# A two-layer diffusion block on one core: the opening re-ordered, GpSimd's arithmetic moved to VectorE, a ring of eight split weight blocks

## What is computed

```python
silu_c, silu_cc = silu(c), silu(c_ctx)
mod   = silu_c  @ w_ada[l] + b_ada[l]      # 2048 -> 3 * 2048: shift, scale, gate
mod_c = silu_cc @ w_ada[l] + b_ada[l]
h  = rmsnorm(x,  norm_g) * (1 + scale)   + shift
hc = rmsnorm(xc, norm_g) * (1 + scale_c) + shift_c
u, v_a, g_a, cq, ckv, kr, g_b, q_c, k_c, v_c, g_c = split_in(h @ w_in)
```

## Time and profile before

| | before |
|---|---|
| runs, us | 1631.42, 1628.64, 1631.72; median 1631.42 |
| profiled execution, span, us | 1630.7 |
| median of the runs less that span, us | 0.7 |
| PE busy | 1526.5 us, 94% |
| DVE busy | 1180.9 us, 72% |
| ACT busy | 684.2 us, 42% |
| POOL busy | 216.7 us, 13% |
| mean granted clock of TensorE | 0.979 |

### The profile page before, as it was taken

How to read it: one execution, slowest core, us unless ns; L and a number is a source line. 1 busy time by engine, 2 the same in 40 slices (tenths; PEclk the granted TensorE clock), 3 DMA queues, 4 the chain that set the end, 5 groups by cost and what they waited for, 6 DMA issues and landing times.

```text
span 1630.7 us, 26688 instructions
## 1 busy us (share of the span) xinstructions
PE 1526.5 (94%) x8082; PEld 1293.1 (79%) x8082; DVE 1180.9 (72%) x2080; ACT 684.2 (42%) x1274; POOL 216.7 (13%) x318
## 2 busy tenths in 40 slices
PE   3688899989999999999999999789989999999998
PEld 2456688878888888877888888678879988888897
DVE  3899788777978974757678887675765656767765
ACT  3766522242332323335462222343545534445554
POOL 1433321102111210100001110021200010200000
PEclk9799999999999999999999999899999999999999
DMA  8778676606665653642106775367736665731374
GB/s 238 241 249 261 232 251 183 191 27 199 174 189 154 209 152 91 173 117 57 42 12 208 240 234 172 95 151 188 240 121 178 172 181 137 229 91 46 106 213 145
DMA packets 318055, 268.62 MB, mean 165 GB/s; under 512 B 37072, under 2 KB 269712, under 8 KB 316944
## 3 DMA queue, kind: packets, MB, share of 16 engines
q1 hardware_dynamic: 296208, 196.23, 42.0%
q0 software_dynamic: 21760, 71.32, 13.7%
HBM read 257.00 MB, written 10.49 MB: 164 GB/s over the span
## 4 chain that ended last, share of the span: by engine, by line
PE 77%; DVE 11%; issue 4%; ACT 3%; DMA 2%; SPq 2%; DVEq 0%; POOL 0%; ACTq 0%; POOLq 0%
PE ps L916 23%; PE ps L918 23%; PE ps L917 23%; DVE w_lo L1305 4%; PE ps L921 2%; DMA ada_w<-in_w_ada 2%; PE ps L1077 1%; SPq L325 1%; ACT w_hi L567 1%; PE ps L1082 1%; PE ps L1081 1%; DVE ada_acc L1360 1%; DMA w_raw<-in_w_ada 1%; DVE prob L1508 1%; SPq L351 1%
## 5 line engine op out<-in xcount | busy, mean ns | idle before, releaser
L567 ACT ACTIVATE w_hi<-w_raw 128x512 fp32r<-128x512 f32 x656 | 406.9, 630 | 603.4 <-PE ps L918 533.6
L1305 DVE TENSOR_TENSOR w_lo<-w_raw,w_hi 128x512 fp32r<-128x512 f32 x656 | 472.0, 734 | 258.7 <-ACT w_hi L567 254.7
L916 PE MATMUL ps<-h_hi,w_lo 128*128 128x512 f32 (+1 forms) x1120 | 390.9, 349 | 3.4 <-DVE vc_lo L1319 1.5
L918 PE MATMUL ps<-h_hi,w_hi 128*128 128x512 f32 (+1 forms) x1120 | 388.2, 347 | 0.0
L917 PE MATMUL ps<-h_lo,w_hi 128*128 128x512 f32 (+1 forms) x1120 | 388.2, 347 | 0.0
L1360 DVE SCALAR_TENSOR_TENSOR ada_acc<-ada_w,c_silu,ada_acc 128x512 f32<-128x512 f32 x448 | 318.4, 747 | 8.9 <-DMA ada_w<-in_w_ada 8.6
L523 POOL DMA_DIRECT2D ada_w<-in_w_ada x256 | 137.4, 537 | 984.7 <-DVE ada_acc L1360 974.9
L916 PEld LDWEIGHTS ps<-h_hi,w_lo 128*128 128x128 f32 x1120 | 212.0, 189 | 31.9 <-issue 3.1
L918 PEld LDWEIGHTS ps<-h_hi,w_hi 128*128 128x128 f32 x1120 | 212.0, 189 | 26.3
L917 PEld LDWEIGHTS ps<-h_lo,w_hi 128*128 128x128 f32 x1120 | 212.1, 189 | 26.0
L1025 PE MATMUL ps<-w_lo,c_st 128*128 128x512 f32 x128 | 62.3, 487 | 36.5 <-DVE w_lo L1305 36.3
(11 more groups left out here) (220 smaller groups left out, 2375.9 us busy)
## 6 DMA issues: line engine op xcount, KB each, us to landing
w_raw<-in_w_in SPq DMA_DIRECT2D x336, 256.0 KB, 3.3
ada_w<-in_w_ada POOLq DMA_DIRECT2D x256, 256.0 KB, 3.6
w_raw<-in_w_ada SPq DMA_DIRECT2D x128, 256.0 KB, 4.2
w_raw<-in_w_out SPq DMA_DIRECT2D x128, 256.0 KB, 4.1
w_raw<-in_w_ukv SPq DMA_DIRECT2D x32, 256.0 KB, 3.1
ada_w<-in_w_in POOLq DMA_DIRECT2D x16, 256.0 KB, 3.9
x_scratch<-z SPq DMA_DIRECT2D x4, 1024.0 KB, 7.6
w_raw<-in_w_uq SPq DMA_DIRECT2D x16, 256.0 KB, 2.9
```

What stands on the lines that cost most here:

```text
L567: act.activation(dst, src, ACT.Copy).then_inc(hi_made, 1)
L916: pe.matmul(dst, a_lo, b_hi, start=first, stop=False)
L918: return pe.matmul(dst, a_hi, b_hi, start=False, stop=last)
L1305: dve.tensor_tensor(dst, src, top.bitcast(F32), ALU.subtract).then_inc(lo_made, 1)
```

## The change

- SP: w_ada blocks 0 to 7 are requested ahead of x and ctx, blocks 8 on right behind them; `load_bias(0)` comes behind v_c's rows.
- Ring: w_ada blocks use 8 split slots (`split_at`: w_hi/w_lo and the new wx_hi/wx_lo), `ADA_RING` = 8; ACT and DVE run `ADA_AHEAD` = 6 blocks ahead, 3 after the opening (`lead`, `led`).
- x: squares, turning and scaling start at block 10 (`X_AT`), the RMS matmul comes at block 20 (`RMS_AT`).
- Chunks: `normed` and xn are gone. DVE's `chunk_scaled` makes tmp = z * a_col * prob at step c (two instructions 128x256), ACT's `chunk_hi` h_hi from tmp and q_whi at c+1, DVE's `chunk_lo` h_lo (two 128x256) and q_wlo at c+3, PE's `q_unit` for the same chunk at c+4, c in (6, 13, 20, 27). The last four chunks and q_units are woven into the first blocks of v_c.
- POOL issues transfers only; the loads of q_c's rows start when x has landed. The mask is one DVE `min` with a table of the largest float or -1e30, behind v_c in both layers.
- The first ada block is added four steps later within v_c; its last four rows come behind the loop.
- The row copy goes to prob row 1 instead of tmp row 3. Groups are Python loops instead of `Fori` loops.

The diff, cut:

```diff
-CHUNK_AT = (4, 11, 18, 25)
+ADA_UNITS = 2 * KT * GROUPS
+ADA_RING, ADA_AHEAD = 8, 6
+CHUNK_AT = (6, 13, 20, 27)
+X_AT, RMS_AT = 10, 20
+def lead(u):
+    return max(min(u + ADA_AHEAD, ADA_UNITS - 1), u + AHEAD)
+def led(u):
+    return range(lead(u - 1) + 1, lead(u) + 1)
...
+        def split_at(u):
+            if u < ADA_UNITS and u % ADA_RING >= RING:
+                return wx_hi[:, u % RING, :], wx_lo[:, u % RING, :]
+            return w_hi[:, u % RING, :], w_lo[:, u % RING, :]
...
# SP
-            for tt in range(4):
-                src = (x if tt < 2 else ctx_in)[0, (tt % 2) * P:(tt % 2 + 1) * P, :]
-                sp.dma_start(x_in[:, tt, :], src).then_inc(x_landed[tt], 16)
...
-            for n in range(RAW):
-                ada_row(0, n)
-            load_bias(0)
...
+            for u in range(RAW):
+                ada_row(u)
+            for tt in range(4):
+                src = (x if tt < 2 else ctx_in)[0, (tt % 2) * P:(tt % 2 + 1) * P, :]
+                sp.dma_start(x_in[:, tt, :], src).then_inc(x_landed[tt], 16)
+            for u in range(RAW, ADA_UNITS):
+                ada_row(u)
...
                         sp.dma_start(x_scratch[:, 4 * g:4 * g + 4, :], z[:, 4 * g:4 * g + 4, :]).then_inc(x_kept, 16)
+                    load_bias(l)
...
# POOL: mask_bias, normed and q_lo are gone
+            pool.wait_ge(x_landed[3], 16)
+            for k in range(KT):
+                q_row(k)
...
# ACT
+                ring = ADA_RING if u < ADA_UNITS else RING
+                if u >= ring or per:
+                    act.wait_ge(unit_done, u - ring + 1 + per * i)
...
+            def chunk_hi(k):
+                act.wait_ge(t_ready, k + 1)
+                for v in range(2):
+                    t = slice(v * SEQ, (v + 1) * SEQ)
+                    ins = act.activation(h_hi[:, k, t], tmp[:, k % 2, t], ACT.Identity, bias=mods[:, v, k:k + 1])
+                ins.then_inc(op_hi, 1)
+                act.wait_ge(ada_in[k % 4], 16 * (k // 4 + 1))
+                if k >= 2:
+                    act.wait_ge(q_done, k - 1)
+                act.activation(q_whi[:, k % 2, :], ada_w[:, k % 4, :], ACT.Copy).then_inc(q_hi_made, 1)
+            for u in range(ADA_AHEAD):
+                prep(u)
+            for u in range(ADA_UNITS):
+                g, n = divmod(u, 2 * KT)
+                for ahead in led(u):
+                    prep(ahead)
+                if n % KT == 0 and u:
+                    rows_copy(g, n // KT)
+                if u in (X_AT, X_AT + 1):
+                    x_square(u - X_AT)
+                if 0 <= u - X_AT - 2 < KT:
...
+                if g and n - 1 in CHUNK_AT:
+                    chunk_hi(4 * g - 4 + CHUNK_AT.index(n - 1))
...
# PE
+                pe.matmul(ps[:, bank, :], c_st[:, s, :], top, start=False, stop=s == KT - 1).then_inc(unit_done, 1)
+                if g and n - 4 in CHUNK_AT:
+                    q_unit(4 * g - 4 + CHUNK_AT.index(n - 4))
             turn_rows_of(GROUPS, 0)
-            for c in range(5):
-                q_unit(GROUPS, c)
...
+                    if l == 0 and 1 <= k < 5:
+                        q_unit(KT - 5 + k)
...
# DVE
+            def chunk_scaled(k):
...
+                if k >= 2:
+                    dve.wait_ge(op_ready, k + 1)
+                for v in range(2):
+                    t = slice(v * SEQ, (v + 1) * SEQ)
+                    ins = dve.scalar_tensor_tensor(out=tmp[:, k % 2, t], in0=z[:, k, t], scalar=a_col[:, v, k:k + 1],
+                                                   in1=prob[:, 0, t], op0=ALU.mult, op1=ALU.mult)
+                ins.then_inc(t_ready, 1)
+            def chunk_lo(k):
+                dve.wait_ge(t_ready, k + 1)
+                dve.wait_ge(op_hi, k + 3)
...
+                dve.wait_ge(q_hi_made, k + 1)
+                dve.tensor_tensor(q_wlo[:, k % 2, :], ada_w[:, k % 4, :], q_whi[:, k % 2, :].bitcast(F32), ALU.subtract)\
+                    .then_inc(q_lo_made, 1)
...
+                if g and n in CHUNK_AT:
+                    chunk_scaled(4 * g - 4 + CHUNK_AT.index(n))
+                if g and n - 3 in CHUNK_AT:
+                    chunk_lo(4 * g - 4 + CHUNK_AT.index(n - 3))
...
+                    chunk_scaled(KT - 4)
                     for k in range(KT):
+                        if k < 4:
+                            if k < 3:
+                                chunk_scaled(KT - 3 + k)
+                            chunk_lo(KT - 4 + k)
                         prep_ahead(PLAN["v_c", l]["unit"] + k)
+                        if k == 4:
+                            block = ada_block(l, "v_c")
+                        if k >= 4:
+                            ada_add(block, k - 4)
+                        if 8 <= k < 12:
+                            lo(qc_lo[:, k - 8, :], ps[:, k - 8, :], qc_hi[:, k - 8, :], C_SCALE).then_inc(free[k - 8], 1)
+                    for k in range(KT - 4, KT):
                         ada_add(block, k)
...
                 ada(l, "v_c")
+                dve.wait_ge(bias_in, 16 * ROWS * HEADS_C * (l + 1))
+                near = bias[:, :, :].rearrange("p a (r c) -> p (a r) c", c=GRID_W)
+                dve.tensor_tensor(near, near, cst[:, C_MASK:C_MASK + GRID_W].unsqueeze(1).broadcast_to([P, 32, GRID_W]),
+                                  ALU.min).then_inc(bias_ready, 1)
```

More of the change, by code:

```diff
@@ L604, in _, with x_square @@
                 hi(c_st[:, :, 2 * v], c_silu[:, v * KT:(v + 1) * KT])
-            for c in range(2):
+            def x_square(c):
                 act.wait_ge(x_landed[c], 16)
@@ L659, in _ @@
+            rows_copy(GROUPS, 0)
             hi_n[0] += KT
@@ L661, in _ @@
             t_n[0] = KT
-            act.wait_ge(q_done, KT)
-            for j in range(4):
-                hi(qc_hi[:, j, :], ps[:, j, :], C_SCALE)
             def softmax_exp(j, keys):
@@ L1419, in _ @@
                                               1.0, 0.0, ALU.mult, ALU.add, small[:, 50 + c:51 + c]))
-            for u in range(AHEAD):
+            for u in range(ADA_AHEAD):
                 prep(u)
@@ L1439, in columns_of @@
                                              op0=ALU.add, op1=ALU.mult).then_inc(group_ready, 1)
[L1441 to L1447 removed]
+            def chunk_scaled(k):
+                if k % 4 == 0:
+                    dve.wait_ge(group_ready, k // 4 + 1)
+                if k == 0:
+                    dve.wait_ge(free[7], 1)
+                    for j in range(4):
+                        dve.wait_ge(free[j], KT // 4)
+                if k >= 2:
@@ L1480, in _ @@
-            group(0, 0)
-            group(1, 2 * KT)
-            with dve.Fori(2, GROUPS) as g:
-                group(g, 4 * KT, g - 2, 2 * KT)
+                for v in range(2):
+                    t = slice(v * SEQ, (v + 1) * SEQ)
+                    ins = dve.scalar_tensor_tensor(out=h_lo[:, k, t], in0=tmp[:, k % 2, t], scalar=mods[:, v, k:k + 1],
+                                                   in1=h_hi[:, k, t].bitcast(F32), op0=ALU.add, op1=ALU.subtract)
+                ins.then_inc(op_ready, 1)
@@ new lines, in chunk_lo, with x_scale @@
+                dve.wait_ge(q_hi_made, k + 1)
+                dve.tensor_tensor(q_wlo[:, k % 2, :], ada_w[:, k % 4, :], q_whi[:, k % 2, :].bitcast(F32), ALU.subtract)\
+                    .then_inc(q_lo_made, 1)
+            def x_scale():
+                dve.wait_ge(sq_ready, 2)
+                link(dve.tensor_scalar(small[:, 0:4], small[:, 50:54], 1.0 / D, EPS, ALU.mult, ALU.add))
+                rsqrt(4)
+                for c in range(4):
+                    ins = dve.tensor_scalar(tmp[:, 2, c * P:(c + 1) * P], ident, small[:, 10 + c:11 + c], None, ALU.mult)
+                    if c % 2:
+                        ins.then_inc(sq_sum, 1)
@@ new lines, in _ @@
+            for u in range(ADA_UNITS):
+                g, n = divmod(u, 2 * KT)
+                for ahead in led(u):
+                    prep(ahead)
+                if u in (X_AT, X_AT + 2):
+                    x_square(2 + (u - X_AT) // 2)
+                if u == X_AT + 5:
+                    x_scale()
+                if u == RMS_AT + 3:
+                    dve.wait_ge(job_done, 3)
+                    dve.tensor_copy(prob[:, 0, :], ps[:, 7, :]).then_inc(free[7], 1)
+                if n % KT == 5 and u > KT:
+                    columns_of(g, n // KT)
+                if g and n in CHUNK_AT:
+                    chunk_scaled(4 * g - 4 + CHUNK_AT.index(n))
+                if g and n - 3 in CHUNK_AT:
+                    chunk_lo(4 * g - 4 + CHUNK_AT.index(n - 3))
@@ L1484, in _ @@
             columns_of(GROUPS, 0)
-            for c in range(4):
-                chunk(GROUPS, c)
             hi_n[0] += KT
@@ L1489, in _ @@
             t_n[0] = KT
-            for j in range(4):
-                lo(qc_lo[:, j, :], ps[:, j, :], qc_hi[:, j, :], C_SCALE).then_inc(free[j], 1)
             def nmax(j, keys):
```

245 lines of the change are left out of this document (71 added, 174 removed).

## The result

The changed kernel takes **1667.62 us** (median of 4 runs, 1667.12 to 1668.65) against 1631.57 of the kernel before on the same chip (4 runs, 1628.64 to 1632.32): ratio 1.0221, 95% interval 1.0204 to 1.0239. It is slower, by 36 us. The profiled execution has a span of 1665.2 us against 1630.7; its mean granted clock is 0.963. DVE is busy for 1152.4 us and PE for 1536.9 us, 92% of the span, of which some is the same work at half rate.

A forecast was written before the change was run, and what follows sets the result against it. PE was taken as the bound after the opening, so what the opening gains or loses is kept. Terms -26.9 +26.9 +24.2 +0.5 +7.9 -4.3 = +28.3 on the 1630.7 span gave 1659 us, range 1632 to 1674.

The forecast's parts named there:

- rival A: Main case, all terms as summed: loops longer and clock lowered; 1659 us, own range 1647 to 1670, chance 0.60.
- half rate all through q_unit: Opening loops: the lower clock covers every q_unit whole, +41.5 us, 1672 us in all; chance 0.10.
- The mechanism of the loops: Opening loops: each chunk starts only when the last q_unit is over, and q_unit waits for its own chunk; plus 26.9 us.
- The chain: Path from q_unit round to the next: 10.8 us per ordinary loop, 14.3 per long one; eleven loops 125.8 against 98.9.
- Rival D: Opening loops: ACT and DVE get a chunk ahead of PE, loop 6.94 us, no pauses; 1592 us, chance 0.16.
- The clock term: Opening loops: PE's 4.8 us pauses bring the lower clock, 2.2 us eleven times; plus 24.2 us, ends 0 and 37.
- Rival B: Opening loops: equally long, but pauses too short to lower the clock; 1635 us, chance 0.14.
- The lead-in: Start up to q_unit 0: it comes at 59.1 against 86.0; minus 26.9 us, bounds -22 and -31.
- block 8 starts 26.0 us earlier: Lead-in: bias transfers moved back and x behind eight w_ada blocks, so block 8 is split by 21.3 us.
- The end of v_c: Value projection's end: PE's transposes wait 5.6 us for late ada sums, lower clock costs 2.3; plus 7.9 us; bias issues covered.
- Layer 1: Mask moved from POOL to DVE: stretched h_lo and PE's wait go; minus 4.3 us, ends 0 and -5.
- the rest of v_c: From q_unit 11 to the projection's end: 59.2 us against 58.7 now; plus 0.5 us.

The follow-up runs named there:

- the runs with 5, 4 and the late q_unit: Changed kernel with ADA_AHEAD 5 in place of 6: 1635.31 us; with 4: 1617.94 us; with 6 but q_unit behind block c+9: 1619.24 us.
- filling the pause: Changed kernel with 14 unused matmuls added on PE ahead of each q_unit but the first: 1647.53 us.
- The new opening in its best form: Changed kernel with ada sums spread, bias issued by POOL, x squares early, 5 blocks ahead and q_unit behind block c+6: 1605.49 us (4 runs).

## Why the prediction was right, and where it was off

It gave 1659 (1632 to 1674) and slower a chance of 0.77, chiefly by rival A (0.60): the ring that does not uncouple. The time is 1667.6, within the range; 1635 for "the clock stays up", 1672 for "half rate all through q_unit" and 1592 for "the ring uncouples" stood beside it.

**The mechanism of the loops was right.** It said that each chunk can only start when the last q_unit is over, since split c+13 has the slot of block c+5. The rows at 125.49, 125.98 and 126.64 show that hand-over, and the runs with 5, 4 and the late q_unit remove it. The chain was put at 10.8 us and 14.3; without the clock's part it is 10.48 and 14.13. One part was off: PE's pause was put at 4.8 us in each loop and is 2.1 to 4.9, since PE, at the lower clock, is busy for more of the loop than was counted. Rival D, that DVE would get ahead of PE, needed the slot to be no obstacle: with a lead of 4 it is none, and the loop is then 8 us, not D's 6.9, and does little better than the old one.

**The clock term was mis-sized a little:** +24.2 predicted, 19.9 measured by filling the pause. Rival B (no clock term) falls with it: the pauses did bring the lower level. With the clock kept up the time is 1647.53, where B had 1635, because other terms were put too low. By the Trainium skill, "TensorE: Matmul & The Clock Gate", part on the clock gate, the prediction had this term under 16 us. That does not hold here: 19.9 us are 1.2% of the span.

**The lead-in was the term that failed:** -26.9 predicted, with bounds of -22 and -31, and -19.1 measured, outside the bounds. Block 8 came at 24.38 instead of 21.3: 3.1 us. The windows view of the kernel after, over the stretch in which x and block 8 arrive (columns as above):

```profile
2.50:8.00 5.50, 0.58 (x2) 0.29 (x2) 1.24 (x5) 1.59 (x5) 0.34 (x1) 1.00 0.95 311
8.00:15.00 7.00, 6.23 (x16) 3.79 (x16) 4.78 (x8) 3.79 (x6) 0.00 (x0) 1.00 1.03 401
15.00:22.00 7.00, 0.00 (x0) 0.00 (x0) 0.00 (x0) 0.00 (x0) 0.00 (x0) 0.79 1.00 414
```

The prediction let 399 GB/s run from 2.5 us on. That rate is there from 8 us, and even exceeded, but the first 5.5 us have 311, which is 0.5 MB or 1.2 us less. By 22 us 7.4 MB had moved, more than the 6.9 of tables, eight blocks and x and the 0.25 of block 8, and ACT could copy block 8 only at 22.97. So transfers requested behind it had part of the rate; that is inferred from the sum, no run changes it. Block 32 came at 53.6 instead of 47.3, another 3.2 us late; there PE waits 5.15 us for z behind ACT's squares, which had been priced, with the lower clock, at 2 in all. q_unit 0, another 1.5 us late, is then 7.8 late.

The step "block 8 starts 26.0 us earlier" (22.9 measured) also joins two moves of unlike worth. In the old kernel with the bias transfers moved, block 8 starts at 30.94, 16.4 us earlier, and q_unit 0 no later than in the changed kernel; the rest comes from asking for w_ada ahead of x, and doesn't last until block 32. The rows of the kernel before were misread at one place as well: 74.45 in the earlier trace rows is the first matmul of block 34, two blocks on. Block 32's is

```profile
73.10 0.50 PE L1025 MATMUL ps<-w_lo,c_st 128*128 128x512 f32 x1 [0.41 <-DVE w_lo L1305]
```

so the 24 blocks took 25.8 us before, not 27.1, and take 29.2 after, where 26 had been forecast.

**The end of v_c:** the wait for the sums was 5.6, with "covered; if not, a few us" for the bias transfers. It was 9.25. Without the bias transfers on SP's queue it is 5.42, so the first number was right and "covered" was wrong. SP's timeline of the kernel after shows it:

```profile
235.07 21.45 SPq L343 DMA_DIRECT2D bias<-in_rpb  x16
256.93 4.98 SPq L350 DMA_DIRECT2D w_raw<-in_w_in  x3
```

The bias requests lay 36 us ahead of the projection's end, earlier than the 30 forecast, but k_c's first blocks were only asked for at 256.93, and DVE's splits, with the sums behind them in its order, needed them long before PE did: ACT stood 5.89 us for the first of them, until 266.56, and PE used it at 281.70. Behind the wait the granted clock is 0.50 from 280 to 285 us, and the kernel loses another 2.4 us up to the attention (from +36.6 to +39.0), where 2.3 had been predicted for the lower clock. From q_unit 11 to the transposes there are another 2.0 us beside the wait, where 0.5 stood.

**Layer 1:** -4.3 predicted, -5.0 measured at the start of q_c. The mask on DVE takes 2.28 us, where a square of x took 2.29:

```profile
1124.92 2.28 DVE L1571 TENSOR_TENSOR bias<-bias,cst 128x2048 f32<-128x2048 f32 x1
```

**The sum.** Lead-in +7.8 against the prediction, loops -2.5 for the chain and -4.3 for the clock, the rest of v_c +1.5, its wait +3.7, layer 1 -0.7, and what lies between the marks together +0.7: +6.2, that is +34.5 measured for +28.3. Lead-in, rest and wait were put too low, chain, clock and layer 1 too high. That the total is within about half a per cent is in part luck: terms off by up to 8 us cancel.

**Where the expected gain went.** In the old kernel, moving the bias transfers and the mask is worth 14.7 us (1633.0 to 1618.3, single runs), and 17.3 when the transfers also leave SP's queue (1631.2 to 1613.9). The new opening in its best form adds 8.4 us to that (1613.87 to 1605.49): by the profiles 4.0 up to q_unit 0, 1.6 in the loops, 0.8 up to the transposes and 1.0 behind them. In the form of the change it costs 54 us (1613.87 to 1667.62): q_unit 0 comes at 66.93 against 66.28 there, the loops take 143.2 against 98.8, from q_unit 11 to the transposes it is 69.9 against 63.0, and the lower clock behind that wait takes 2.4. It stays open which engine or which part of the change brings these 8 us, the freed POOL among them: no run here separates them. Whether the last wait of 1.44 us and the 12.2 us of the long loops can be removed wasn't tried.

## What to carry to other kernels

When a producer runs ahead through a ring, don't only count the slots: for each step write down which slot it needs, who frees it, and what long step that engine has in front. A larger lead in one in-order program can need a slot whose release stands behind the last long step of the consumer, and then less ahead is faster: here 4 blocks ahead beat 5, and 5 beat 6. And once such a chain makes PE pause, its price is not the pause alone: here the same loop cost 24.4 us by waiting and 19.9 us more by the clock.

Sixteen small transfers were the costliest thing on their queue here. Ask of each place what stands behind them there, and which engine's in-order program that holds up; where two causes of one wait lie side by side, mend both before judging either.
